# A two-layer transformer block on one core: another order for the prologue, and six rows of a matrix-vector product on TensorE

## What is computed

```python
def hybrid_layer(x, c, rel_table, w_ada, b_ada, pre_g, post_g, w_in, sink,
                 w_pool_grp, pool_scale, w_br_attn, w_br_pool, w_merge, b_merge, w_out):
    mod = jax.nn.silu(c) @ w_ada + b_ada
    shift, scale, gate = jnp.split(mod, 3, axis=-1)
    h = rmsnorm(x, pre_g) * (1.0 + scale[:, None]) + shift[:, None]
    proj = h @ w_in
    q, k, v, gate_a, u, gate_p = jnp.split(proj, SPLIT_POINTS, axis=-1)
    y_a = windowed_gqa(q, k, v, rel_table, sink) * jax.nn.silu(gate_a)
    y_p = multiscale_pool(u, w_pool_grp, pool_scale) * jax.nn.silu(gate_p)
    ...
    return x + gate[:, None] * rmsnorm(o, post_g)
```

## Time and profile before

| | us |
|---|---|
| median of 3 runs (2445.57 to 2456.84) | 2450.28 |
| profiled execution | 2450.23 |
| its span | 2448.3 |
| TensorE busy | 2286.6 (93%) |
| VectorE busy | 1742.4 (71%) |
| ScalarE busy | 1125.4 (46%) |
| first gemm product starts | 125.45 |

### The profile page before, as it was taken

The page is one execution under the profiler, slowest core; times in us unless marked ns, Lnnn a source line. Parts: engine busy times, 40 slices in busy tenths (PEclk is TensorE's granted clock), DMA queues, the critical chain, the costliest instruction groups (busy, mean ns, idle before and its releaser), DMA issues.

```text
span 2448.3 us, 31291 instructions
## 1 busy us (share of the span) xinstructions
PE 2286.6 (93%) x12880; PEld 1973.2 (81%) x12880; DVE 1742.4 (71%) x2015; ACT 1125.4 (46%) x1432; POOL 81.2 (3%) x105
## 2 busy tenths in 40 slices
PE   2499999999998899999999989998999999999998
PEld 1388888888787778888888878787888888888887
DVE  5877867767876677767777788877777777774443
ACT  1243446564445554543455633355444444444443
POOL 1000000001000000000011100000000000000000
PEclk7599999999999999999999999999999999999999
DMA  9967877877883756668876778884555555565552
GB/s 356 411 240 260 287 237 271 295 254 255 307 286 108 274 174 224 228 220 308 277 237 232 254 264 317 312 292 138 189 184 183 185 188 189 189 217 179 173 188 103
DMA packets 245090, 580.56 MB, mean 237 GB/s; under 512 B 11850, under 2 KB 14718, under 8 KB 240596
## 3 DMA queue, kind: packets, MB, share of 16 engines
q1 hardware_dynamic: 232320, 535.86, 63.5%
q0 software_dynamic: 11296, 40.20, 4.7%
q10 hardware_dynamic: 1332, 2.51, 0.3%
HBM read 557.55 MB, written 20.97 MB: 236 GB/s over the span
## 4 chain that ended last, share of the span: by engine, by line
PE 78%; DVE 11%; DMA 7%; ACT 2%; issue 1%; ACTq 0%; DVEq 0%; SPq 0%
PE gemm L1699 46%; PE gemm L1700 23%; DVE w_lo L1059 3%; PE gemm L1703 3%; DMA mod_stage<-in_w_mod 3%; DMA w_stage<-in_w_ada 3%; DVE mod_acc L1053 2%; PE gemm L1702 1%; PE extra L1499 1%; DMA w_stage<-in_w_in 1%; PE extra L1492 1%; ACT w_hi L701 1%; PE extra L1631 1%; DVE mod_acc L1038 1%; PE extra L1607 1%
## 5 line engine op out<-in xcount | busy, mean ns | idle before, releaser
L1699 PE MATMUL gemm<-operand_main,w_hi 128*128 128x512 f32 x4311 | 1560.6, 403 | 49.7 <-DVE operand_main L1110 17.8
L1700 PE MATMUL gemm<-operand_main,w_lo 128*128 128x256 f32 x4311 | 1217.4, 282 | 0.0
L1059 DVE TENSOR_TENSOR w_lo<-w_stage,w_hi 128x1024 fp32r<-128x1024 f32 x736 | 861.2, 1212 | 449.9 <-ACT w_hi L701 449.5
L701 ACT ACTIVATE w_hi<-w_stage 128x1024 fp32r<-128x1024 f32 x736 | 732.2, 1044 | 767.3 <-PE gemm L1700 726.7
L1699 PEld LDWEIGHTS gemm<-operand_main,w_hi 128*128 128x128 f32 x4311 | 820.4, 190 | 241.6 <-issue 28.3
L1700 PEld LDWEIGHTS gemm<-operand_main,w_lo 128*128 128x128 f32 x4311 | 824.4, 191 | 13.5
L1053 DVE SCALAR_TENSOR_TENSOR mod_acc<-mod_stage,c_silu,mod_acc 128x1024 f32<-128x1024 f32 x210 | 267.1, 1301 | 49.3 <-DMA mod_stage<-in_w_mod 43.1
L1699 PE MATMUL gemm<-ffn_hidden,w_hi 128*128 128x512 f32 x688 | 242.9, 397 | 0.0
L1699 PE MATMUL gemm<-operand_attn,w_hi 128*128 128x512 f32 x480 | 180.4, 415 | 15.3 <-DVE proj L1365 10.7
L1700 PE MATMUL gemm<-ffn_hidden,w_lo 128*128 128x256 f32 x688 | 192.5, 280 | 0.0
L1699 PEld LDWEIGHTS gemm<-ffn_hidden,w_hi 128*128 128x128 f32 x688 | 129.1, 188 | 29.5
(11 more groups left out here) (211 smaller groups left out, 1459.3 us busy)
## 6 DMA issues: line engine op xcount, KB each, us to landing
w_stage<-in_w_in SPq DMA_DIRECT2D x128, 1024.0 KB, 6.2
mod_stage<-in_w_mod SPq DMA_DIRECT2D x192, 512.0 KB, 5.9
w_stage<-in_w_up SPq DMA_DIRECT2D x88, 1024.0 KB, 5.0
w_stage<-in_w_down SPq DMA_DIRECT2D x44, 1024.0 KB, 5.0
w_stage<-in_w_ada SPq DMA_DIRECT2D x32, 1024.0 KB, 11.2
w_stage<-in_w_merge SPq DMA_DIRECT2D x32, 1024.0 KB, 5.5
w_stage<-in_w_out SPq DMA_DIRECT2D x32, 1024.0 KB, 7.6
mod_stage<-in_w_ada SPq DMA_DIRECT2D x32, 512.0 KB, 5.7
```

What stands on the lines that cost most here:

```text
L701: return nc.scalar.activation(o, i_, f, **kw)
L1059: tt(WL[:, slot_of(n), c0:c1], WST[:, slot_of(n), c0:c1], WH[:, n % HIS, c0:c1].bitcast(F32), ALU.subtract)\
L1699: mm(G[:, m, :], hi, x_of(k), start=(k == 0), stop=False)
L1700: ins = mm(G[:, m, T:2 * T], lo, x_of(k)[:, 0:T], start=False, stop=False)
```

## The change

- **Order.** The identity is loaded by SP. Rows use four of the five slots, slab 0 is loaded into the fifth behind the first four rows, and the wait for x and the vectors is gone. The storing of x, of the bias lines and the loads of the pool tables start after two slabs are used. Small vectors behind the first pack are turned after the norm's sums.
- **Bias lines by one product.** One product with the 33 x 8 table as the weight gives all eight lines, one copy takes them to SBUF, and one DMA stores them, each repeated 128 times (2 MB from eight partitions).
- **Rows on TensorE.** Rows 18, 20, 22, 24, 26 and 28 are no longer accumulated by VectorE. TensorE takes each 128 x 128 block of the row from the stage as the weight and the silu column as the single moving column, and accumulates in PSUM; the column sums of what VectorE accumulated are added to the same place. Row 31 comes in two halves, and the scale is finished in two halves (`scale_half`). The memsets of both accumulators go; rows 0 and 16 are plain products.
- **Splits.** Slab 0 is split ahead of the last rows, slabs 1 to 3 inside the loop that makes the operand tiles.
- **Phases.** The first in phase is put ahead of u0 and u1; the rows of the gate's vector (part 2) and the pool hooks are dealt anew over the phases.

```diff
...
-        phases.append(Phase("u0", 0, [one(2560)]))
-        phases.append(Phase("u1", 0, [one(3072)], mod=(2, 0, 3)))
-        for n, c in enumerate((0, 512, 1024, 1536)):
-            phases.append(Phase("in", n, [one(c)], mod=(2, 3 + 2 * n, 2), slots=(0, 2),
-                                hooks={0: [("pool_sum", n)], 1: [("pool_mix", n)], 2: [("pool_out", n)]}))
+        pool = lambda n: {0: [("pool_sum", n)], 1: [("pool_mix", n)], 2: [("pool_out", n)]}
+        phases.append(Phase("in", 0, [one(0)]))
+        phases.append(Phase("u0", 0, [one(2560)], mod=(2, 0, 2), slots=(0, 2)))
+        phases.append(Phase("u1", 0, [one(3072)], mod=(2, 2, 2), slots=(0, 2)))
+        for n, c in enumerate((512, 1024, 1536)):
+            phases.append(Phase("in", n + 1, [one(c)], mod=(2, (4, 6, 8)[n], (2, 2, 3)[n]), slots=(0, 2, 1), hooks=pool(n)))
         for i in range(2):
             phases.append(Phase("in_gates", i, [one(2048 + 1536 * i)], mod=((2, 11, 3), (2, 14, 2))[i],
-                                post=[("mod_end", 2)] if i else []))
+                                hooks={} if i else pool(3), post=[("mod_end", 2)] if i else []))
...
+        ROW_SLOTS = RAW - 1
+        LAST_ROW = MOD0_ROWS - 1
+        PE_ROWS = (18, 20, 22, 24, 26, 28)
+        pe_rows = sem("rows_by_pe")
+
+        def rows_done(eng, t):
+
+            if t in PE_ROWS:
+                eng.wait_ge(pe_rows, PE_ROWS.index(t) + 1)
+            else:
+                eng.wait_ge(mod0_rows, rows_by_dve(t) + 1)
+
+        def rows_by_dve(t):
+            return sum(r not in PE_ROWS for r in range(t))
+
...
+            def load_slab(n):
+
+                ph, g, q = slabs[n]
+                if 0 < n < RAW:
+                    rows_done(sp, MOD0_ROWS - RAW + n)
+                elif n:
+                    sp.wait_ge(slab_used, n - RAW + 1)
+                src = g.w.rearrange("(c q) n -> q c n", q=P)[:, q * QUAD:(q + 1) * QUAD, g.col:g.col + g.cols]
+                sp.dma_start(WST[:, slot_of(n), 0:g.size].rearrange("q (c n) -> q c n", c=QUAD), src).then_inc(w_landed[slot_of(n)], 16)
+
+            sp.dma_start(IDENT[:, :], A["k_ident"]).then_inc(start["ident_in"], 16)
             for t in range(MOD0_ROWS):
                 w, part = mod_w[t // 16]
-                free_slot(t)
-                if t == 4:
-                    sp.wait_ge(start["vec_in"], 16 * sum(len(p) for p in packs[1:]))
-                    sp.wait_ge(start["x_in"], 16)
+                if t == ROW_SLOTS:
+                    load_slab(0)
+                if t >= ROW_SLOTS:
+                    rows_done(sp, t - ROW_SLOTS)
                 src = w.rearrange("(c q) n -> c q n", q=P)[t % 16, :, part * D:(part + 1) * D]
...
+                if t < LAST_ROW:
+                    sp.dma_start(WST[:, t % ROW_SLOTS, :], src).then_inc(w_landed[t % ROW_SLOTS], 16)
+                else:
+                    sp.dma_start(WST[:, t % ROW_SLOTS, 0:D // 2], src[:, 0:D // 2]).then_inc(half_row_in, 16)
+                    sp.dma_start(WST[:, t % ROW_SLOTS, D // 2:D], src[:, D // 2:D]).then_inc(w_landed[t % ROW_SLOTS], 16)
...
+            pool.wait_ge(slab_used, 2)
             pool.wait_ge(xt_copied, 8)
             pool.dma_start(resid.rearrange("t q n -> q t n"), PROJ[:, XT0:XT0 + KT, :]).then_inc(start["x_t_stored"], 16)
 
-            for h in range(HEADS1):
-                pool.wait_ge(line_copied, h + 1)
-                pool.dma_start(lines[h, 0:P * LINE].rearrange("(q k) -> q k", q=P), LINEB[:, h % 2, :])\
-                    .then_inc(start["lines_stored"], 16)
+            pool.wait_ge(line_copied, 1)
+            pool.dma_start(lines[:, 0:P * LINE].rearrange("h (q k) -> h q k", q=P),
+                           LINE8[:, :].unsqueeze(1).broadcast_to([HEADS1, P, LINE])).then_inc(start["lines_stored"], 16)
             pool.wait_ge(vec_copied, NP)
-            pool.wait_ge(line_copied, HEADS1)
-            pool.wait_ge(start["lines_stored"], 16 * HEADS1)
+            pool.wait_ge(start["lines_stored"], 16)
...
-                        for first_slab in range(3):
-                            split_hi(first_slab)
+                        for pack in range(1, NP):
+                            copy_vectors(pack)
+                        act.wait_ge(line_mm, 1)
+                        activate(LINE8[:, :], X[0][0:HEADS1, :], ACT.Copy).then_inc(line_copied, 1)
+                        split_hi(0)
                     shift = (0, 3, 6)[k] * KT
-                    act.wait_ge(modv_ready, (2, 5, 8)[k])
+                    act.wait_ge(modv_ready, (1, 5, 8)[k])
                     positive(act, slab_used, ph.slab0)
                     for t in range(KT):
-                        if t == 9:
+                        if k == 0 and t in (5, 10):
+                            split_hi(t // 5)
+                        if k and t == 9:
                             split_hi(ph.slab0 + 3)
                         act.wait_ge(scaled, KT * k + t + 1)
                         activate(HL[:, t, 0:T], WORK[:, t % 8, :], ACT.Identity, bias=MODV[:, shift + t:shift + t + 1]).then_inc(op_hi, 1)
+                    if k == 0:
+                        split_hi(3)
...
+            def first_rows(r0, r1):
+                for t in range(r0, r1):
+                    if t in PE_ROWS:
+                        continue
+                    acc = (MACC, MACC1)[t // 16]
+                    for c0, c1 in ((0, D),) if t < LAST_ROW else ((0, D // 2), (D // 2, D)):
+                        if t == LAST_ROW and c0 == 0:
+                            dve.wait_ge(half_row_in, 16)
+                        else:
+                            dve.wait_ge(w_landed[t % ROW_SLOTS], 16 * (t // ROW_SLOTS + 1))
+                        positive(dve, mod0_rows, rows_by_dve(t))
+                        row = WST[:, t % ROW_SLOTS, c0:c1]
+                        if t % 16 == 0:
+                            ins = ts(acc[:, c0:c1], row, CSI[:, 0:1], None, ALU.mult)
+                        else:
+                            ins = stt(acc[:, c0:c1], row, CSI[:, t % 16:t % 16 + 1], acc[:, c0:c1], ALU.mult, ALU.add)
+                        ins.then_inc(mod0_rows if c1 == D else half_row, 1)
...
+            first_rows(0, 25)
             norm_rs(0)
-            for p in range(2):
-                stage_mod_end(p)
+            stage_mod_end(0)
+            first_rows(25, 28)
+            split_lo(0)
+            first_rows(28, MOD0_ROWS)
+
+            def scale_half(half):
+
+                c0, c1 = half * KT // 2, (half + 1) * KT // 2
+                g = col["pre_norm_g"]
+                dve.wait_ge((half_summed, mod_summed)[half], (1, 2)[half])
+                tt(MODV[:, KT + c0:KT + c1], X[2 - half][:, c0:c1], COL[:, mod_b[1] + c0:mod_b[1] + c1], ALU.add)\
+                    .then_inc((half_modv, modv_ready)[half], 1)
+                dve.wait_ge((half_modv, modv_ready)[half], (1, 2)[half])
+                stt(AFF[:, c0:c1], MODV[:, KT + c0:KT + c1], 1.0, COL[:, g + c0:g + c1], ALU.add, ALU.mult)\
+                    .then_inc((half_affine, affine)[half], 1)
+                dve.wait_ge((half_affine, affine)[half], 1)
...
+                    if k == 0:
+                        scale_half(0)
+                    else:
+                        if k == 1:
+                            affine_of(k)
+                        split_lo(ph.slab0 + 2)
                         norm_rs(norm_of[("prep_h", k)])
-                    dve.wait_ge(affine, k + 1)
+                        dve.wait_ge(affine, k + 1)
                     for s in range(KT + 2):
-                        if s == 11:
+                        if k == 0 and s == 4:
+                            scale_half(1)
+                        if k == 0 and s in (7, 12, 17):
+                            split_lo(s // 5)
+                        if k and s == 11:
...
+            for n in range(1, NP):
+                turn_vectors(n)
+            pe.wait_ge(vec_copied, NP)
+            pe.wait_ge(start["line_in"], 32)
+            mm(X[0][0:HEADS1, :], TABX[:, :], OHOT[:, :], start=True, stop=True).then_inc(line_mm, 1)
+            pe.wait_ge(start["const_in"], 32)
             mod_end(0)
-            mod_end(1)
+            pe.wait_ge(c_ready, 2)
+            for r in PE_ROWS:
+                pe.wait_ge(w_landed[r % ROW_SLOTS], 16 * (r // ROW_SLOTS + 1))
+                for t in range(KT):
+                    ins = mm(X[2 - t // 8][:, t:t + 1], WST[:, r % ROW_SLOTS, t * P:(t + 1) * P], CSI[:, r % 16:r % 16 + 1],
+                             start=(r == PE_ROWS[0] and t % 8 == 0), stop=False, skip_group_check=True)
+                ins.then_inc(pe_rows, 1)
+            for half in range(2):
+                pe.wait_ge((half_row, mod0_rows)[half], (1, MOD0_ROWS - len(PE_ROWS))[half])
+                for t in range(8 * half, 8 * half + 8):
+                    ins = mm(X[2 - half][:, t:t + 1], MACC1[:, t * P:(t + 1) * P], ONES[:, 0:1], start=False, stop=(t % 8 == 7),
```

(12 more changed lines are left out.)

77 lines of the change are left out of this document (18 added, 59 removed).

## The result

| | us |
|---|---|
| median of 4 runs (2477.84 to 2483.27) | 2479.31 |
| kernel before beside it, 4 runs (2445.57 to 2456.84) | 2448.56 |
| ratio, with its 95% interval | 1.0121 [1.0102, 1.014] |
| profiled execution, and its span | 2477.84, 2476.1 |
| TensorE busy | 2322.6 |

The change costs 1.2%, about 30 us, where I had forecast a gain of 12. The page gives the granted clock and the chain in the form of the earlier trace rows.

A forecast was written before the change was run, and what follows sets the result against it. TensorE bounds the kernel, so an earlier first gemm product counts fully: 125.45 - 111.4 = 14.0 us gained, less 0.6, 0.7 and 0.7, is 12.0, giving 2438.2 us. Range 2425 to 2445 us.

The forecast's parts named there:

- The bound and the value of an earlier start: Prologue: whatever comes before the first gemm product is worth its full length if TensorE then runs without holes; 14.0 us gained.
- The splits that stand inside and behind the prep: First gemm phase: low half 3, moved behind the last tile, comes at 130.5 where TensorE wants it at 129.9; 0.6 us lost.
- 0.7 us for a late evacuation of the first pair: After the first four slabs: VectorE makes low half 5 before it evacuates the first pair; 0.7 us lost.
- The stream: Prologue row loads: the hole at 19 to 26 us goes, rows come every 2.47 us, row 15 is summed at 54.6 us.
- The term of 25.0 us for row 4: Prologue stream: 8.9 MB ahead of and with row 4, 4.3 MB by 14 us, the rest at 424 GB/s; in at 25.0 us.
- my upper bound of 57: Prologue: row 15 summed at 57 us if the stream ran at 400 GB/s.
- Six rows at 7.0 us: Prologue on TensorE: each row's sixteen one-column products take 7.0 us at clock 0.50, within bounds of 3.7 to 7.0.
- The 56.8 us that I had set for the eight blocks: TensorE behind row 15: shift sum, six rows and last sum, 7.0 us each plus hand-over; gemm starts at 111.4 us.
- The late line store at no cost: After the prologue: one 2.1 MB store from eight partitions, results wanted near 182 us, blocking TensorE only from 199; no loss term.
- line store starves the pool: Rival, 4%: pool tables behind the line store come late; slower from 74 us of store, 2535 us in all at 159.
- Redealt rows: Third pool phase, now with three modulation rows: VectorE needs 23.8 us against 22.6, first pair evacuated late; 0.7 us lost.
- The six rows as such: Prologue: moving six rows to TensorE makes it the bound, with VectorE idle half the time; gemm starts at 111.4 us.

The follow-up runs named there:

- no_line_store: Changed kernel with each bias line stored once (16 KB in all), without the 128-fold repetition, for timing alone: 2441.05 us, ratio 0.9967.
- lines_from_dram: Changed kernel with the lines stored once to DRAM, then repeated 128 times by one DRAM to DRAM transfer, repetition outermost: 2443.97 us, ratio 0.9971.
- store_early: Changed kernel with its eight-partition line store issued as soon as the lines are copied (40.25 us), ahead of resid: 2469.21 us, ratio 1.0081.
- lines_one_each: Changed kernel with the line store as eight stores, one per head from one partition each, 128 repetitions outermost: 2514.74 us, ratio 1.0262.
- late_lines_vector: Changed kernel with all 32 rows on VectorE, DRAM line repetition in first in_gates, fourth pool group in second, one gate row moved to u1: 2431.10 us, 0.9933.

## Why the prediction was wrong

**The bound and the value of an earlier start: right.** The first phase ended 10.4 us earlier for a gemm that started 10.7 us earlier. The splits that stand inside and behind the prep cost 0.3 us of it (24.4 us from the first product to the mark against 24.05), where I had set 0.6. The next term, 0.7 us for a late evacuation of the first pair, did not show: where the store is out of the way, in no_line_store and lines_from_dram, the phase behind takes the usual 22.6 us.

**The stream: right in kind, 3.4 us off.** The hole went, as forecast. The term of 25.0 us for row 4 measured 27.9. Of that, 1 us is that 3.9 MB had moved by 14 us (183 GB/s x 8 us + 407 x 6) where I carried over 4.3 from the earlier trace rows, and 1 us that the stream then ran at 380 to 405 GB/s instead of 424. The last one is bytes: by 27.9 us the stretches sum to 9.4 MB, 0.5 more than the 8.9 that I had counted ahead of and with row 4. Part of row 5 is a likely candidate, not a shown one. Row 15 was therefore summed at 58.0 instead of 54.6, just outside my upper bound of 57.

**Six rows at 7.0 us: right.** Measured 6.85 each, back to back, at 0.50, which is 1.2 GHz, after 20 us in which TensorE had done nothing. The 56.8 us that I had set for the eight blocks, counted from 58.0, give 114.8, and 114.73 was measured. In that agreement two small errors cancel: the blocks took 2.0 us less in all, and TensorE waited 1.9 us for VectorE ahead of the last sum. The gemm's start was off by 3.3 us, all of it inherited from the stream. The rule of the Trainium skill that I weighed (page "TensorE: Matmul & The Clock Gate", section "What's actually happening") would have had the clock rise: here it did not in 48 us of unbroken one-column work, nor when wide products stood between.

**The late line store at no cost: the step that failed.** The sum has no term for it. I asked only when its *result* is wanted (182 us for the tables, 199 for TensorE) and not what the transfer does to others while it runs. The two phases beside it took 35.9 us longer, and with the repetition from DRAM all but about 1 us of that is gone. The rival "line store starves the pool" was on the right transfer with the wrong mechanism: it charged only the time by which the store exceeds 62 us, through the pool tables, and at 51 us nothing. The price came through the slab loads and the gate's rows.

The length itself I had priced at 51 us, "like eight median ones", and it measured 51.8. That is luck. The eight stores before read 128 partitions each and took 6.4 us apiece, while the DMA engines moved 424 GB/s in all. The new store reads eight partitions and is slow with half of the DMA engines idle. I took the one kind for the other because the bytes are the same. The rows of before could not show this price; store_early does, where the new store in the old place starts the gemm 23 us later. Beside the slab loads it costs more, 35 us against 25.

The Trainium skill has a line that spoke against this change and that I did not weigh: page "DMA: Bandwidth & Descriptors", section "Why a DMA increments its semaphore by 16 and not by 1", says that a transfer is carried by the largest number of engines, at most sixteen, that divides its outermost dimension on both sides, so one of size eight gets at most eight. The trace agrees in part: the share is 0.50 to 0.53 from 150 to 170 us. But lines_one_each kept all sixteen busy and was slower, so the rule does not give the price.

**Redealt rows: mis-sized.** The term of 0.7 us measured 5.2. I also had its place wrong: the fourth pool group went to the first in_gates phase, which has three rows as well, so two three-row pool phases follow each other. My schedule added up VectorE's work (23.8 us, and against 22.6, where a pool phase takes 24.2) and left out that it waits for the halves of its rows, 3.6 us in the first of these phases. That these waits make the long phase fits the trace and is not shown by a run of its own.

**The six rows as such** cost instead of gaining. The prediction said that TensorE becomes the bound of the prologue, and stopped there; with VectorE alone the gemm starts 6.7 us earlier. A kernel without both mistakes (late_lines_vector, 2431.1) beats the kernel before by 0.67% and the change by 48 us.

**What stays open:** why eight neighbouring partitions read at 40 GB/s and eight spread ones at 63 (2.1 MB over 51.8 and 33.3 us), and how much of the starvation is engines held and how much the reads from the partitions. A store from all 128 partitions in the new place was not run. Also whether the 5 us of the long phase in late_lines_vector can be had.

## What to carry to other kernels

A transfer that nobody waits for still has a price: ask which loads share the DMA engines with it during its whole length, and how far ahead the reader of those loads is. In these runs repeating 2.1 MB out of eight SBUF partitions cost 35 us more than storing it once and repeating it from DRAM, with a dimension of 128 outermost. A length taken from another transfer of the same bytes holds only if its source and shape are the same too. And before work is moved to an idle engine, write down that engine's new total against the old bound: six rows of 7 us on a TensorE at 1.2 GHz were longer than the VectorE time that they saved.

## What the runs showed of the hardware that I had not expected

- 2.1 MB stored from SBUF: 51.8 us from eight neighbouring partitions, 33.3 us from eight partitions sixteen apart, and about 50.6 us in the median for each of eight overlapping stores from one partition each (84 us for all). From DRAM: 13.3 us with 128 outermost, 21.2 us with eight outermost.
- A busy share of the DMA engines says nothing of bytes: 0.97 to 1.00 at 39 to 47 GB/s in lines_one_each, 1.04 at 395 GB/s in lines_from_dram.
- The granted clock stayed at 0.50 for 48 us of unbroken one-column products, and also when a 128 x 512 product started every 1.28 us between them.
